# Keys' inverse norms folded into the delta rule's per-token numbers, and the other norms spread in one pass

## The reference, cut to what matters

```python
def l2_normalize(x):
    return x * lax.rsqrt(jnp.sum(x * x, axis=-1, keepdims=True) + 1e-6)

# branch A, per head of 128 values
o = rms_norm(o, subln_w) * (1.0 - lambda_init)

# branch B, per head of 128 values, behind convolution and SiLU
qc = l2_normalize(qc) * (DN_HEAD_DIM ** -0.5)
kc = l2_normalize(kc)
beta = jax.nn.sigmoid(beta_logit)
g = -jnp.exp(A_log) * jax.nn.softplus(a_logit + dt_bias)
# chunk_gated_delta_rule: gc = cumsum(g) within a chunk
decay = where(incl, exp(gc_i - gc_j), 0)
kb = k * beta
A = where(strict, (kb @ k.T) * decay, 0);  T = inverse(I + A)
u = T @ (v * beta);  w = T @ (kb * exp(gc))
qk = (q @ k.T) * decay
k_dec = k * exp(gc_last - gc)
```

## Time and profile before

| | |
|---|---|
| median of 3 runs | 693.03 us (692.12 to 693.23) |
| profiled execution | 693.96 us, span 692.2 us |
| mean granted clock of TensorE | 0.954 |
| busy PE, DVE, ACT, POOL | 610.1, 339.8, 266.0, 43.6 us |
| spreads on PE (L925) | 48 records for 24 spreads, 392 ns each, from 209.0 to 245.7 us |
| scalings of keys and queries (L1817) | 16, 412 ns each; of meta keys (L1816) 8, 162 ns each |
| HBM read | 154.12 MB, 422 GB/s in the expert stage |

### The profile page before, as it was taken

How to read it: one execution, slowest core, us unless ns; L and a number is a source line. 1 busy time by engine, 2 the same in 40 slices (tenths; PEclk the granted TensorE clock), 3 DMA queues, 4 the chain that set the end, 5 groups by cost and what they waited for, 6 DMA issues and landing times.

```text
span 692.2 us, 14248 instructions
## 1 busy us (share of the span) xinstructions
PE 610.1 (88%) x5829; PEld 506.7 (73%) x5829; DVE 339.8 (49%) x746; ACT 266.0 (38%) x592; POOL 43.6 (6%) x92
## 2 busy tenths in 40 slices
PE   4999999999999998999899799997887957749764
PEld 3999998898998888999799799985544514325341
DVE  6344449999878768564755368624211111011103
ACT  5245448677776435235332946323101100101003
POOL 8300000000000001100310100000000000000000
PEclk9999999999999999999999989998999979788989
DMA  9954551332333332221321158898999999999992
GB/s 286 298 163 134 175 183 62 123 107 78 122 122 122 123 105 80 62 66 59 97 90 62 62 175 277 359 422 331 387 420 422 419 421 422 422 422 422 420 401 95
DMA packets 71296, 156.03 MB, mean 225 GB/s; under 512 B 7234, under 2 KB 56500, under 8 KB 59460
## 3 DMA queue, kind: packets, MB, share of 16 engines
q1 hardware_dynamic: 70048, 155.06, 60.4%
q10 hardware_dynamic: 1188, 0.12, 0.2%
HBM read 154.12 MB, written 1.05 MB: 224 GB/s over the span
## 4 chain that ended last, share of the span: by engine, by line
PE 59%; DMA 17%; DVE 15%; issue 4%; ACT 3%; DVEq 0%; SPq 0%; ACTq 0%
PE bank L801 28%; DMA arena<-in_expert_w_down_dram 13%; PE bank L1226 5%; PE bank L982 5%; PE bank L1204 4%; DMA arena<-in_expert_w_gate_dram 4%; DVE w_lo L300 3%; PE bank L786 3%; DVE arena L1789 2%; PE bank L960 2%; PE bank L1189 2%; PE bank L925 2%; DVE arena L1828 1%; ACT w_hi L295 1%; PE bank L1236 1%
## 5 line engine op out<-in xcount | busy, mean ns | idle before, releaser
L801 PE MATMUL bank<-uT_hi,w_hi 128*128 128x272 f32 (+1 forms) x568 | 172.8, 304 | 5.6 <-DVE w_lo L300 3.9
L801 PE MATMUL bank<-uT_lo,w_hi 128*128 128x272 f32 (+1 forms) x568 | 163.4, 288 | 0.0
L801 PE MATMUL bank<-uT_hi,w_lo 128*128 128x272 f32 (+1 forms) x568 | 163.2, 287 | 0.0
L300 DVE TENSOR_TENSOR w_lo<-arena,w_hi 128x1024 fp32r<-128x1024 f32 x88 | 108.7, 1237 | 56.8 <-ACT w_hi L295 56.3
L801 PEld LDWEIGHTS bank<-uT_hi,w_hi 128*128 128x128 f32 x568 | 108.7, 191 | 10.1 <-issue 8.3
L801 PEld LDWEIGHTS bank<-uT_lo,w_hi 128*128 128x128 f32 x568 | 108.9, 192 | 1.4 <-issue 0.5
L801 PEld LDWEIGHTS bank<-uT_hi,w_lo 128*128 128x128 f32 x568 | 108.8, 192 | 0.0
L295 ACT ACTIVATE w_hi<-arena 128x1024 fp32r<-128x1024 f32 x88 | 92.2, 1052 | 0.4 <-DMA arena<-in_w_in_dram 0.3
L1226 PE MATMUL bank<-arena 128*32 128x512 f32 x256 | 39.4, 768 | 30.0 <-DMA arena<-in_expert_w_down_dram 28.5
L1204 PE MATMUL bank<-arena 128*32 128x256 f32 x1024 | 58.9, 389 | 4.9 <-DMA arena<-in_expert_w_gate_dram 4.9
L1204 PEld LDWEIGHTS bank<-arena 128*32 128x32 f32 x1024 | 33.5, 112 | 27.6 <-issue 6.8
(11 more groups left out here) (344 smaller groups left out, 1028.3 us busy)
## 6 DMA issues: line engine op xcount, KB each, us to landing
arena<-in_w_in_dram SPq DMA_DIRECT2D x36, 1024.0 KB, 5.2
arena<-in_expert_w_gate_dram SPq DMA_DIRECT2D x32, 1024.0 KB, 22.1
arena<-in_expert_w_up_dram SPq DMA_DIRECT2D x32, 1024.0 KB, 23.1
arena<-in_expert_w_down_dram SPq DMA_DIRECT2D x28, 1024.0 KB, 19.8
arena<-in_w_branch_attn_dram SPq DMA_DIRECT2D x4, 1024.0 KB, 5.1
arena<-in_w_branch_dn_dram SPq DMA_DIRECT2D x4, 1024.0 KB, 5.4
arena<-in_w_out_dram SPq DMA_DIRECT2D x4, 1024.0 KB, 5.4
arena<-in_expert_w_down_dram SPq DMA_DIRECT2D x8, 512.0 KB, 15.9
```

Of the source, the lines that this page charges most:

```text
L300: nc.vector.tensor_tensor(w_lo[q % NSPLIT], src, w_hi[q % NSPLIT].bitcast(F32), ALU.subtract).then_inc(w_lo_ready, 1)
L801: last = pe.matmul(ps[:, 0:b.shape[2]], a[:, c, :], b[:, c, :], start=(c == 0 and i == 0), stop=(c == NC - 1 and i == 2))
```

## The change

The keys are no longer scaled. `SPREAD` keeps queries and attention heads, so sixteen spreads are left, two to a slot in slots 22 to 25. The roots of the sums are made on 96 and 64 rows instead of 24, since the row of ones that makes the sums (`one_of`) now has three ones 32 apart, so that each sum appears in rows i, 32 + i and 64 + i. A third pass on ACT writes `rs_halves`, a copy rounded to fp32r; DVE then turns its rows 32 to 63 into the low halves. `two_of` has columns with ones in rows i and 32 + i, so one fp32r product adds high and low half and spreads them. Rows 64 to 95 stay logarithms. For the keys, PE transposes `rs_rows` into bank 7 in slot 22, DVE copies the columns of the keys (`key_columns`), PE puts the meta tokens' numbers on the meta chunk's partitions in slot 23, and DVE folds all into `nbk`, `nbegc`, `kdec` and `ngc` in slot 24 (`fold_keys`). POOL copies the unscaled meta keys and sets more constants.

```diff
-        SPREAD = [H + h for h in range(H)] + list(range(H)) + [2 * H + h for h in range(H)]
-        N_DN = 2 * H
+        SPREAD = list(range(H)) + [2 * H + h for h in range(H)]
+        N_DN = H
@@
-            return SPREAD[4 * (m - 22):min(4 * (m - 21), N_DN)] if m >= 22 else []
+            return SPREAD[2 * (m - 22):2 * (m - 21)] if m >= 22 else []
@@ POOL
-            pool.memset(one_of[:, P - 1:P], 1.0)
+            for i in range(3):
+                pool.memset(one_of[:, P - 1 + 32 * i:P + 32 * i], 1.0)
+            for row, value in ((31, EPS), (47, EPS * P), (63, EPS)):
+                link(select(c_mean_eps, c_mean_eps, [[0, 1]], ALU.is_ge, value, row, -1))
+            for row, value in ((31, -0.5 * math.log(P)), (39, 0.0), (47, 0.5 * math.log(P) + math.log(1.0 - LAMBDA_INIT))):
+                link(select(c_rs, c_rs, [[0, 1]], ALU.is_ge, value, row, -1))
+            pool.tensor_tensor(pair_f, ident[:, 0:32], ident[:, 32:64], ALU.add).then_inc(pair_ready, 1)
...
+            pool.wait_ge(silu_ready, 2 * H)
+            pool.tensor_copy(dkT_meta, dkT[:, :, 0:META]).then_inc(k_meta, 1)
@@ PE, spread(k)
                 if k == 0:
-                    pe.wait_ge(rs_ready, 1)
+                    pe.wait_ge(rs_halved, 1)
...
-                pe.matmul(spread_bank(k)[:, 0:L], ident[:, SPREAD[k]:SPREAD[k] + 1].broadcast_to([P, P]), rs_rows,
+                pe.matmul(spread_bank(k)[:, 0:L], two_of[:, SPREAD[k]:SPREAD[k] + 1].broadcast_to([P, P]), rs_halves,
                           start=True, stop=True).then_inc(spread_ready, 1)
@@ PE, slots
+                if m == 22:
+                    pe.wait_ge(rs_ready, 1)
+                    for t in range(TT):
+                        pe.transpose(bank[7][:, t * P:(t + 1) * P], rs_rows[:, TOKENS[t]], ident)
+                    pe.transpose(bank[7][0:META, 2 * P:3 * P], rs_rows[:, 0:META], ident).then_inc(k_turned, 1)
+                if m == 23:
+                    pe.wait_ge(k_own, 1)
+                    pe.matmul(bank[7][:, 3 * P:3 * P + 2 * H], spread16[0:META, :], kc_meta[0:META].rearrange("p a h -> p (a h)"),
+                              start=True, stop=True).then_inc(k_spread, 1)
@@ ACT, roots()
-                link(act.activation(rs_rows[0:NSS, :], bank[7][0:NSS, 0:L], ACT.Ln, bias=c_mean_eps[0:NSS, :]))
-                act.activation(rs_rows[0:NSS, :], rs_rows[0:NSS, :], ACT.Exp, scale=-0.5, bias=c_rs[0:NSS, :]).then_inc(rs_ready, 1)
+                link(act.activation(rs_rows[0:96, :], bank[7][0:96, 0:L], ACT.Ln, bias=c_mean_eps[0:96, :]))
+                link(act.activation(rs_rows[0:64, :], rs_rows[0:64, :], ACT.Exp, scale=-0.5, bias=c_rs[0:64, :]))
+                act.activation(rs_halves, rs_rows, ACT.Copy).then_inc(rs_ready, 1)
@@ ACT, slots
+                if m == 2:
+                    act.wait_ge(pair_ready, 1)
+                    act.activation(two_of, pair_f, ACT.Copy)
@@ DVE, scale_by(i)
-                    dst = (dqT if i < H else dkT)[:, h, :]
-                    if i >= H:
-                        tt(dkT_meta[:, h, :], dst[:, 0:META], ps[:, 0:META], ALU.mult)
-                    last = tt(dst[:, META:L], dst[:, META:L], ps[:, META:L], ALU.mult)
+                    last = tt(dqT[:, h, META:L], dqT[:, h, META:L], ps[:, META:L], ALU.mult)
@@ DVE
+            def key_columns():
+                dve.wait_ge(k_turned, 1)
+                for a in range(2):
+                    k0 = 64 * a + H
+                    dve.tensor_copy(kc_meta[0:META, a, :], bank[7][0:META, 2 * P + k0:2 * P + k0 + H])
+                    last = dve.tensor_copy(kcols[:, a, 0:2 * H].rearrange("p (t h) -> p t h", t=TT),
+                                           bank[7][:, 0:2 * P].rearrange("p (t k) -> p t k", t=TT)[:, :, k0:k0 + H])
+                last.then_inc(k_own, 1)
+
+            def fold_keys():
+                dve.wait_ge(k_spread, 1)
+                for a in range(2):
+                    link(dve.tensor_tensor_reduce(tmp17[:, 0:H], bank[7][:, 3 * P + a * H:3 * P + (a + 1) * H], own_head, 1.0, 0.0,
+                                                  ALU.mult, ALU.add, kcols[:, a, own]))
+                tt(nbk, nbeta, kcols[:, 0, :], ALU.mult)
+                tt(nbegc, nbegc, kcols[:, 0, :], ALU.mult)
+                tt(kdec, kdec, kcols[:, 0, :], ALU.mult)
+                link(stt(ngc, kcols[:, 1, :], -0.5, ngc, ALU.mult, ALU.add))
@@ DVE, slots: at the head of slot 21; behind the scalings of slots 22 and 24
+                    dve.wait_ge(rs_ready, 1)
+                    tt(rs_halves[32:64, :], rs_rows[32:64, :], rs_halves[32:64, :].bitcast(F32), ALU.subtract).then_inc(rs_halved, 1)
...
+                if m == 22:
+                    key_columns()
+                if m == 24:
+                    fold_keys()
```

More of the change, by code:

```diff
@@ L111, in hybrid_block @@
         S = at(spare + 4 * SEQ, H, P)
+        NCOL = 2 * H + 1
         ident, ones, tri, strict, causal_add = (new(P) for _ in range(5))
@@ L117, in hybrid_block @@
         one_of = new(2 * P - 1)
+        kcols, kc_meta, nbk = new(2, NCOL), new(2, H), new(NCOL)
+        top[0] = -(-top[0] // 8) * 8
+        two_of = rounded("two_of", top[0], 1, 32)[:, 0, :]
+        pair_f = new(32)
         c_rs, c_mean_eps = new(1), new(1)
@@ L125, in hybrid_block @@
         ssq, rstd = new(4), new(4)
-        NCOL = 2 * H + 1
         blog, alog, dtb, eA, beta, g, sp, tmp17 = (new(NCOL) for _ in range(8))
@@ L156, in hybrid_block @@
         rs_rows = at(FLOATS - FLOATS % 8 - L, L)
+        rs_halves = rounded("rs_halves", FLOATS - FLOATS % 8 - 2 * L, 1, L)[:, 0, :]
         cbuf = new(2, L + CONV - 1)
@@ L229, in hybrid_block @@
         vec_T, vec_ready = sem("vec_T"), sem("vec_ready")
+        rs_halved, pair_ready, k_meta, k_turned, k_own, k_spread = (
+            sem(n) for n in ("rs_halved", "pair_ready", "k_meta", "k_turned", "k_own", "k_spread"))
         ssq_ready, var_ready, rstd_ready, xn_ready = sem("ssq_ready"), sem("var_ready"), sem("rstd_ready"), sem("xn_ready")
@@ L956, in dn @@
                     pe.wait_ge(gate_cols, 2)
+                    pe.wait_ge(k_meta, 1)
                 def each(o, lhsT, rhs, start=True, stop=True):
@@ L995, in dn @@
                         if c == 1:
-                            pe.wait_ge(qk_ready, NSS)
+                            pe.wait_ge(qk_ready, len(SPREAD))
                     each(X, lambda h: col(h).broadcast_to([P, P]), lambda h: lower)
@@ L1918, in dn @@
                     of_pe()
-                    done(tt(piece(2, 0), Zs, per_head(nbeta, Q), ALU.mult))
+                    done(tt(piece(2, 0), Zs, per_head(nbk, Q), ALU.mult))
                 elif s == "s2":
@@ L1973, in dn @@
                     of_pe()
-                    done(tt(piece(5, 0)[Q:P], Zs[Q:P], per_head(nbeta, Q)[Q:P], ALU.mult))
+                    done(tt(piece(5, 0)[Q:P], Zs[Q:P], per_head(nbk, Q)[Q:P], ALU.mult))
                 elif s == "t3":
```

1 line of the change is left out of this document (added).

## The result

| | before | changed |
|---|---|---|
| median of the timed comparison | 693.78 us (692.0 to 695.57, 20 runs) | 689.69 us (687.76 to 693.7, 20 runs) |
| ratio, 95% interval | 1 | 0.9944 (0.9932 to 0.9956) |
| profiled execution | 693.96 us, span 692.2 us | 689.17 us, span 687.4 us |

The change makes the kernel faster by 4.1 us in the medians, 3.9 by the ratio; 687.9 was forecast. Two later comparisons gave ratios of 0.9955 and 0.994. All 35 runs of the changed kernel have their median at 689.54.

The account below looks back on a forecast made before the run. PE's products bound the kernel up to about 425 us, then the expert-weight stream. Gains of 2.8 us by the meta chunk's first step and 2.3 from singles make 5.1, taking the median 693.03 to 687.9 us; range 686.0 to 689.8.

Parts of the forecast that it names:

- ACT 0.45 later: Slots 20 and 21: a third pass on the roots and a waited-out Exp put ACT's evacuation 0.45 us later.
- Tile 23: Split tile in slots 22 to 25: waits for DVE's low half, starts 0.45 us later than before, at 211.6.
- Tile 24: Next split tile: held by DVE's low half, starts 1.37 us behind it, 215.6 for 216.4, 0.8 gained.
- The folding: DVE in slot 24: two reductions, three products and one that is waited for, 0.9 us together.
- The meta chunk's first step: PE step waiting for the last of the queries' scalings: starts at about 223.9 for 226.73, 2.8 us gained.
- The singles: Eight spreads standing singly between the meta chunk's steps; seven on the chain at 0.33 us each bring 2.3 us.
- given back: Rival: singles bring nothing and part of the 2.8 goes, or one pass costs two; 1 us left, 692.0; 9%.
- The wait behind the eighth: PE's wait before the product at 250.50: the eighth single's shorter spread only lengthens it, by some 0.3 us.
- POOL's constants: Rival: six new selects at 1.2 us each leave nearly 7 us spare; at 4 us each, 697.8; 3%.
- The clock: Rival: PE's waits around slot 22 bring the granted clock down at tile 23; gain only 2.6, 690.4; 12%.
- the wait of 3.9 us: PE idle 3.91 us until 397.53, then clock 0.50 from 398 to 402: the source of 2.5 us lost.
- The expert stream: SP's expert weight loads, from 424.8 us when PE has used up the ring's last weights: start 5 us earlier.

Follow-up runs that it names:

- e1_again: The changed kernel again, no edit, profiled a second time: median 690.62 us, ratio 0.9955.
- e3_dve_copy: Changed kernel with the rounding pass of the roots moved from ACT to DVE: median 690.38 us, ratio 0.9942.
- e4_one_pass: Against the kernel before, one part alone: all 24 spreads in one pass, keys scaled as before, no folding: median 691.19 us, ratio 0.9963.
- e8_fill_look: Second profile of the changed kernel with 18 idle products in PE's two waits of slot 22: 689.31 us.
- e6_order: Changed kernel with the rounding pass on DVE and ACT and PE reordered in slots 21, 22 and 25: 687.85 us, ratio 0.9909.
- e9_order_again: The kernel with the pass on DVE and ACT and PE reordered, run again unchanged: 687.6 us, ratio 0.9912.
- e5_fold_only: Against the kernel before, one part alone: keys folded, sixteen spreads left in float32, no third pass: median 692.49 us, ratio 0.9977.

## Why the prediction was right

Point by point, with e1_again's profile, which had no fall in the stretch and starts it 203.34 - 202.14 = 1.20 us earlier. To compare with the prediction's times, 1.20 is added.

- **ACT 0.45 later.** L1376 predicted at 206.0; 204.85 + 1.20 = 206.05. DVE's subtraction ran in idle time as costed:

```profile
204.51 0.43 ACT L1470 ACTIVATE rs_halves<-arena 128x272 fp32r<-128x272 f32 x1
204.85 0.38 ACT L1376 ACTIVATE arena<-bank 128x272 f32<-128x272 f32 x1
```

```profile
204.97 0.43 DVE L1925 TENSOR_TENSOR rs_halves<-arena,rs_halves 32x272 fp32r<-32x272 f32 x1 [1.49 <-ACT rs_halves L1470]
...
209.04 1.23 DVE L307 TENSOR_TENSOR w_lo<-arena,w_hi 128x1024 fp32r<-128x1024 f32 x1 [1.22 <-ACT w_hi L302]
...
213.00 1.20 DVE L307 TENSOR_TENSOR w_lo<-arena,w_hi 128x1024 fp32r<-128x1024 f32 x1
...
219.52 0.16 DVE L1914 CUSTOM_DVE_ANT_0 arena<-bank,arena 128x8 f32<-128x8 f32 x1
...
220.20 0.17 DVE L1919 SCALAR_TENSOR_TENSOR arena<-arena 128x17 f32<-128x17 f32 x1
220.41 0.43 DVE L1880 SCALAR_TENSOR_TENSOR gateT<-arena 128x256 f32<-128x256 f32 x1
```

- **Tile 23** predicted at 211.6; 210.37 + 1.20 = 211.57, on the low half. e3_dve_copy shows the 0.45 to be ACT's pass.
- **DVE from low half to low half**: 4.0 predicted; 213.00 - 209.04 = 3.96. **Tile 24** predicted at 215.6, found at 215.63; **tile 25** gains 1.8 by the prediction, 221.27 - 219.51 = 1.76 in the profiles.
- **What holds tile 24** is not what the prediction says, though the time is. The low half is done at 213.00 + 1.20 = 214.20, by the prediction's 1.37 the tile could start at 214.37, and it starts at 214.43. In the chain of e1_again PE has no idle time between tiles 23 and 24: it is PE's own work, 3.26 us of products and 0.79 of transposes, spreads and the small product, that ends 0.06 us later than DVE's. So DVE and PE meet there, a faster DVE would gain nothing at this tile, and a slow tile 23 is paid in full. Ahead of tile 25 PE waits 0.39 us, and there it is the low half.
- **The folding**: 0.9 predicted, from 219.52 to the gate's evacuation at 220.41, 0.89. The start behind an operation that is waited for lies 0.21 later (220.20 to 220.41), the starts of those that are not lie 0.08 to 0.10 apart. The Trainium skill (VectorE: DVE Perf Modes, The DRAIN you can't avoid) holds, from a measurement of eight copies, that a semaphore between DVE operations costs nothing extra; the trace doesn't agree for operations as small as these.
- **The meta chunk's first step** predicted at 223.9; 222.75 + 1.20 = 223.95. But it waits for something else than I wrote:

```profile
222.75 0.71 PE L986 MATMUL bank<-arena 128*128 128x128 f32 x4 [0.90 <-ACT arena L1404]
```

  It is released by ACT's evacuation of the values, not by the queries' scalings, whose last ends at 221.88 + 0.74 = 222.62, 0.13 ahead of the step. The time was right, the reason only one of two that meet there.
- **The singles**: seven at 0.33 make 2.3; measured 4.92 - 2.78 = 2.14, for PE waits once for DVE in between, 0.17 us in the first profile's row of PE. The prediction had named PE waiting for DVE between the meta steps as a sign of being wrong; that, and nothing more, is what the rival "given back" had in it:

```profile
232.21 0.45 PE L1008 MATMUL bank<-arena 64*64 64x64 f32 x8 [0.17 <-DVE arena L1981]
```

- **The wait behind the eighth** single: 1.15 us before, 1.47 now, 0.3 longer as written.
- **POOL's constants.** POOL's rows in the first profile after, and PE's first use:

```profile
14.63 6.42 POOL L636 TENSOR_SCALAR_AFFINE_SELECT arena<-arena 128x1 f32<-128x1 f32 x9
...
24.26 2.07 POOL L715 TENSOR_SCALAR arena<-arena 128x144 f32<-128x144 f32 x3
```

```profile
34.17 0.39 PE L857 MATMUL bank<-arena 16*128 16x16 f32 x2
```

  Nine selects took 6.42 us, 0.71 each where I had 1.2. The constants are done before the row at 24.26, which belongs to the attention's biases, so ten microseconds are left to the first use at 34.17: the rival that would have made the kernel slower is refuted.
- **The clock** is where the prediction was off. I gave it 12%, 2.5 us, and one outcome for the kernel. It fell at tile 23 in one of four profiles of the changed kernel and in two of the variants, at a price of 1.46 us in the changed kernel (1.5 and 2.5 in the variants, by tile 23's products). What failed is its price, taken from the wait of 3.9 us, and its form, a lasting property of the kernel. The idle times, 1.26 to 1.27 and 1.07 to 1.21 us with 1.05 us of products between them, were there in all four. The Trainium skill (TensorE: Matmul & The Clock Gate, A second HAM failure mode) says that repeated short idling can bring the clock down; the trace agrees so far as a fall follows such waits in some executions and not in others, but no run shows that the waits are its cause.
- **The expert stream**: its first load was predicted 5 us earlier. Counted from the table load it starts 221.5 us behind in the kernel before, 218.7 in the first profile after and 217.0, 216.9 and 216.5 in the other three: 2.7 us earlier with the fall at tile 23, 4.5 to 5.0 without it.

The sum for the stretch was 5.1; the stretch gives 4.9 in three profiles and 3.45 in the one with the fall. So the mechanism held in the main: the gain is what ACT and DVE let through, and not the 8.4 us that PE loses.

The time itself came out less well than the range makes it look. Measured are 689.69 us for a forecast of 687.9, only 0.1 inside the upper bound of 689.8; e1_again's median, 690.62, is outside. That the time fell into the range is in part luck. Of the 1.8 us, 0.75 come from the start: the forecast counts from the median of three runs, 693.03, and twenty gave 693.78. The other 1.0 is gain that the medians don't show, 4.1 for 5.1. The stretch without a fall explains 0.2 of it.

The falls of the clock are the likely reason for the rest, but this isn't shown. In the mean over the four profiles of the changed kernel those at tile 23 and at the `ya_hi` tile take 0.25 x 1.46 + 0.5 x 1.45 = 1.1 us from the 4.9. The first piece and the rest give as much back, though: they are 0.5 and 0.7 us shorter in the mean than in the kernel before, mostly, by the profiles, through the level of the clock in the opening and through how long it fell behind the wait of 3.9 us. So the four profiled executions average 688.7, 5.2 under the two of the kernel before, and all four lie under the median of the 35 runs, 689.54. What made most of the timed executions slower than these has no profile.

The kernel before had neither fall in two profiles. With 7 of 12 in the other profiles, chance alone gives no fall at the `ya_hi` tile in two about once in six. If that is luck, the change is worth more than the medians say; if the change makes that fall likelier, it is a real price. Each timed run has its mean granted clock on record: 49 of the kernel before have 0.948 to 0.959, 0.9534 in the mean, the 35 of the changed one 0.943 to 0.954, 0.9507 in the mean. So the falls vary in the kernel before too. The difference of 0.0027 is about what one fall of 3.4 us at 0.50 makes in 690 us (1.7 / 690 = 0.0025), but a fall in the opening that only the changed kernel's profiles record (last section) makes just as much, so I can't settle it.

## What to carry to other kernels

Count what leaves an engine, but pay out only what its partner lets through: here PE lost some 8.4 us of products and the stretch gained 4.9, because the halves of the weights come from DVE and ACT in their own time; intervals between two operations of that partner, added up from its own rows, were good to 0.15 us. When an engine is relieved and starts to wait, look at what makes the operand it waits for: moving one pass from ACT to DVE gave another 0.45 us, and reordering ACT and PE around the late half 0.5 more, for no work saved. And before a difference of 1 or 2 us between two profiles is explained, cut both at fixed instructions and look at each piece's granted clock.

## What the runs showed of the hardware

- The clock's fall behind a wait is not a function of the wait's length. 2.42 to 2.46 us ahead of the `ya_hi` tile were followed by it in seven profiles of fourteen; two waits in a row ahead of tile 23, of 0.80 to 1.3 and 1.07 to 1.3 us, in three of six (the four of the changed kernel, e3_dve_copy, e4_one_pass). None of the other eight profiles, in which one of these waits is under 0.6 us or both are filled, has a fall there; if all fourteen executions were alike, chance would put all three falls among those six about once in eighteen. The wait of 3.9 us had a fall in every profile. In the table's six profiles the rest took 294.5 to 294.7 us where that fall lasted 6.8 us, 293.6 to 293.9 where 3.4; in e4_one_pass and e8_fill_look it took 294.7 and 294.8 with a fall of 3.4, so this one fall isn't all of it.
- In the opening a granted clock of 1.00 is not full speed. The first products of slot 0 in the kernel before and in the changed one:

```profile
14.84 2.15 PE L827 MATMUL bank<-uT_hi,w_hi 128*128 128x272 f32 x8 [1.80 <-ACT uT_hi L1391]
```

```profile
14.74 1.32 PE L842 MATMUL bank<-uT_hi,w_hi 128*128 128x272 f32 x8 [1.99 <-ACT uT_hi L1417]
```

  PEclk has 1.00 from 14 to 18 us in the first, and eight products take 2.15 us; in the second it falls to 0.50 between 15 and 16 us, and they take 1.32. One product every 0.24 us is the pace at 0.50 (0.23 in tile 23 of the first profile after), so the durations and not PEclk tell the level there. The 24 products of this kind took 5.54 us (14.84 to 20.38) and 4.61 (14.74 to 19.35), which is most of the 1 us by which the changed kernel reaches the table load earlier in three of its four profiles. It has nothing to do with the change: e6_order and e9_order_again, one kernel, need 4.61 and 5.44 us for them.
- One fp32r product of 272 columns costs 0.13 us in a row (24 in 3.19 us), a float32 product of the same size 0.46 (two in 0.92 in slot 23 of e5_fold_only).
